# Prompt attention: the outputs of two heads leave PSUM together

## The reference

```python
s = (einsum('bqhd,bkhd->bhqk', qn, k_nope) + einsum('bqhr,bkr->bhqk', qr, k_rope)) * ATTN_SCALE
s = where(mask, s, -inf)
p = softmax(s)
return einsum('bhqk,bkhd->bqhd', p, v)          # head size 128, 256 queries
```

## Time and profile before

| | us |
|---|---|
| median of 3 runs (lowest, highest) | 1997.17 (1993.77, 1998.15) |
| the profiled execution's own time | 1997.47 |
| its span, first to last instruction | 1995.4 |
| PE busy | 1962.7 (98%) |
| DVE busy | 1092.1 (55%) |
| ACT busy | 761.0 (38%) |
| mean granted TensorE clock | 0.995 of full speed |
| the loop of the prompt's attention | from 608.4 to 673.9 |

### The profile page before, as it was taken

How to read it: one execution, slowest core, us unless ns; L and a number is a source line. 1 busy time by engine, 2 the same in 40 slices (tenths; PEclk the granted TensorE clock), 3 DMA queues, 4 the chain that set the end, 5 groups by cost and what they waited for, 6 DMA issues and landing times.

```text
span 1995.4 us, 33957 instructions
## 1 busy us (share of the span) xinstructions
PE 1962.7 (98%) x13378; PEld 1938.4 (97%) x13378; DVE 1092.1 (55%) x1464; ACT 761.0 (38%) x834; POOL 45.0 (2%) x188
## 2 busy tenths in 40 slices
PE   8999999999999999999999999999999999999996
PEld 7999999999998799999999999999999999999996
DVE  6865344333335764355556555555556555565656
ACT  5356542332246654233333232332323333333334
POOL 0002000000000000000000000000000000000000
PEclk9999999999999999999999999999999999999998
DMA  7444444444444388454444434444444444343442
GB/s 247 145 150 168 153 147 147 147 147 148 149 175 161 129 284 278 154 201 149 152 153 145 165 137 159 147 147 147 147 148 148 152 153 151 134 164 142 152 147 103
DMA packets 59575, 318.15 MB, mean 159 GB/s; under 512 B 6466, under 2 KB 6658, under 8 KB 26882
## 3 DMA queue, kind: packets, MB, share of 16 engines
q1 hardware_dynamic: 58866, 313.15, 44.2%
q10 hardware_dynamic: 656, 4.27, 0.5%
HBM read 313.08 MB, written 4.32 MB: 159 GB/s over the span
## 4 chain that ended last, share of the span: by engine, by line
PE 96%; ACT 2%; DVE 2%; issue 0%; DMA 0%; DVEq 0%; SPq 0%; ACTq 0%
PE ps L1342 95%; ACT w_hi L469 0%; PE ps L1628 0%; DVE w_lo L816 0%; ACT sq L795 0%; ACT y_gain L796 0%; DVE sq L816 0%; DMA xT<-in_x 0%; DVE y_gain L816 0%; ACT sm L672 0%; DVE neg_max L1109 0%; DVE sm L1103 0%; ACT pt L469 0%; DVE scale_in L883 0%; PE ps L1574 0%
## 5 line engine op out<-in xcount | busy, mean ns | idle before, releaser
L816 DVE TENSOR_TENSOR w_lo<-w_raw,w_hi 128x2048 fp32r<-128x2048 f32 (+1 forms) x270 | 610.2, 2260 | 459.2 <-ACT w_hi L469 459.0
L1342 PE MATMUL ps<-h_hi,w_hi 128*128 128x320 f32 x2512 | 742.0, 308 | 11.0 <-ACT w_hi L469 11.0
L469 ACT ACTIVATE w_hi<-w_raw 128x2048 fp32r<-128x2048 f32 (+1 forms) x271 | 509.1, 1879 | 630.4 <-PE ps L1342 630.0
L1342 PE MATMUL ps<-h_lo,w_hi 128*128 128x320 f32 x2512 | 740.9, 309 | 0.0
L1342 PEld LDWEIGHTS ps<-h_hi,w_hi 128*128 128x128 f32 x2512 | 473.0, 188 | 11.6 <-ACT w_hi L469 11.2
L1342 PEld LDWEIGHTS ps<-h_lo,w_hi 128*128 128x128 f32 x2512 | 471.5, 188 | 0.2
L1342 PE MATMUL ps<-h_hi,w_lo 128*128 128x320 f32 x2512 | 393.6, 308 | 0.0
L1342 PEld LDWEIGHTS ps<-h_hi,w_lo 128*128 128x128 f32 x2512 | 374.8, 187 | 0.0
L1342 PE MATMUL ps<-hid_hi,w_hi 128*128 128x320 f32 x704 | 216.6, 308 | 1.9 <-DVE x L816 1.9
L1342 PE MATMUL ps<-hid_lo,w_hi 128*128 128x320 f32 x704 | 216.5, 308 | 0.0
L1342 PE MATMUL ps<-hid_hi,w_lo 128*128 128x320 f32 x704 | 216.5, 308 | 0.0
(11 more groups left out here) (226 smaller groups left out, 1763.6 us busy)
## 6 DMA issues: line engine op xcount, KB each, us to landing
w_raw<-in_slabs SPq DMA_DIRECT2D x253, 1024.0 KB, 4.8
w_raw<-in_cache_t SPq DMA_DIRECT2D x64, 288.0 KB, 3.8
c_raw<-in_cache SPq DMA_DIRECT2D x56, 256.0 KB, 4.7
w_whole<-in_slabs SPq DMA_DIRECT2D x4, 1024.0 KB, 8.3
xT<-in_x SPq DMA_DIRECT2D x4, 640.0 KB, 7.4
x_again<-in_x ACTq DMA_DIRECT2D x1, 2560.0 KB, 9.5
out_y<-y_gain SPq DMA_DIRECT2D x4, 640.0 KB, 3.2
c_last<-in_cache SPq DMA_DIRECT2D x8, 256.0 KB, 4.4
```

Source lines behind the costliest of these rows:

```text
L469: return nc.scalar.activation(out, in_, ACT.Copy)
L816: return nc.vector.tensor_tensor(out, a, b, op)
L1342: return nc.tensor.matmul(out, a, b, start=start, stop=stop, **kw)
```

## The change

ACT copies the outputs of two heads, banks 6 and 7, by one instruction in even iterations, and DVE subtracts for two heads by one instruction in odd ones; the value product of head h waits until the pair before its own has been taken.

```diff
@@ ACT
-                if i >= 3:
-                    h = i - 3
-                    act.wait_ge(pv_done, h + 1)
-                    copy(o_hi[:, h, 0:NP], ps[:, 6 + h % 2, 0:NP]).then_inc(ohi_done, 1)
+                if i >= 3 and i % 2 == 0:
+                    h = i - 4
+                    act.wait_ge(pv_done, h + 2)
+                    copy(o_hi[:, h:h + 2, 0:NP], ps[:, 6:8, 0:NP]).then_inc(ohi_done, 1)
@@ DVE
-                if i >= 4:
-                    h = i - 4
-                    dve.wait_ge(ohi_done, h + 1)
-                    tt(o_lo[:, h, 0:NP], ps[:, 6 + h % 2, 0:NP], o_hi[:, h, 0:NP], ALU.subtract).then_inc(olo_done, 1)
+                if i >= 4 and i % 2 == 1:
+                    h = i - 5
+                    dve.wait_ge(ohi_done, h // 2 + 1)
+                    tt(o_lo[:, h:h + 2, 0:NP], ps[:, 6:8, 0:NP], o_hi[:, h:h + 2, 0:NP], ALU.subtract
+                       ).then_inc(olo_done, 2)
@@ PE
                     if h >= 2:
-                        pe.wait_ge(olo_done, h - 1)
+                        pe.wait_ge(olo_done, h - h % 2)
```

## The result

| | before | changed |
|---|---|---|
| median of 4 runs (lowest, highest), us | 1997.14 (1993.77, 1998.15) | 2017.83 (2009.94, 2018.86) |
| ratio, 95% interval | | 1.0101 [1.0088, 1.0115] |
| profiled execution: own time, span | 1997.47, 1995.4 | 2018.27, 2016.2 |
| mean granted clock, as a share of full speed | 0.995 | 0.989 |
| from the loop's first scores to the first product behind it, us | 673.87 - 608.35 = 65.5 | 695.74 - 607.77 = 88.0 |

The kernel became 20.7 us slower (1.0%). The forecast was 2014 us in a range of 2006 to 2028.

A forecast was written before the change was run, and what follows sets the result against it. PE, busy 98% of the span, was taken as the bound. Stalls and tail less waits given back made +10.9 us, two clock falls +5.8: +16.7 on 1997.5, forecast 2014 us, range 2006 to 2028.

The forecast's parts named there:

- The stall and its place: PE's value product of an even head waits for DVE's pair, behind the same iteration's masked scores: 2.37 us, six times.
- The sum at full clock: Loop and tail without clock falls: six stalls +14.2, tail +3.1, today's waits given back -3.9 and -2.5; +10.9 us.
- The tail: Last heads: PE waits 1.4 us at i = 17 and 1.7 us after the last product, +3.1 us.
- The saving: Merged subtractions save DVE 0.15 us a pair, 1.2 over the loop; nothing up to i = 8, later at most 1.2.
- What stands behind the moved instructions: Work queued on ACT and DVE behind the moved copies and subtractions shifts only by tenths of a us.
- The clock: In the loop, the granted clock falls at two of the six new stalls, 2.9 us each: +5.8 us.
- Rival (b): Clock falls at four to six of the loop's stalls, +27 to +30 us in all, up to 2027; chance 0.23.
- The fall behind the loop: Today's clock fall after the tail's two waits was left as it is, because the tail's waits stay alike.
- one to three falls: The forecast's own case: one to three clock falls at the loop's stalls, 2011 to 2018 us; chance 0.41.
- Rival (a): Same stalls in the loop but the clock holds, no fall: 2008 us; chance 0.30.
- (c): Not slower: PE reaches the even head's value product after the wait would end, only -0.8 saved, 1996.4 us; chance 0.03.
- (d): Half of the stalls absorbed where DVE is the bound: +5, 2002 us; chance 0.03.

The follow-up runs named there:

- filled kernel: Changed kernel with ten matmuls of unused result ahead of PE's wait at each even head from 2 to 12, filling the stalls; 2005.53 us.
- ACT's pair alone: Kernel before with only ACT's copy merged; DVE subtracts head by head in its old places and PE has the old wait; 2003.35 us, ratio 1.0036.
- changed again: The changed kernel run once more with nothing altered, for the spread of its runs; 2016.2 us, ratio 1.0096.
- pair first: Changed kernel with DVE's subtraction of the pair moved to the head of the odd iteration, ahead of the wait for the scores; 1999.32 us.
- other work first: Changed kernel with PE's latent queries (i = 5, 7) and next stage's scores (i = 11, 15) put ahead of the value product and its wait; 2002.16 us.

## Why the prediction was right, and where it was off

- **The stall and its place.** Forecast 2.37 us at each of six even heads; measured 2.3 to 2.4 by the matmul rows, 2.48 from start to start in iteration 5. Moving the pair's subtraction ahead of the masked scores removed four of them, and one changed wait made them without any merge. Right.
- **The sum at full clock.** +10.9, from +14.2 and +3.1 less 3.9 and 2.5. The filled kernel measures it: +10.7 in the loop. The tail was forecast at 1.4 and 1.7 us, and is 1.25 and 1.57. Right. (By its own terms the upper bound is 14.2 + 3.1 - 2.8 - 2.3 = 12.2 and not 12.0, and its terms make eight waits of PE and not nine; the changed kernel has eight, six of 2.3 to 2.4 us. Five of them stand in the list of waits under ACT's `pt`, by the coincidence named above.)
- **The saving.** A pair's subtraction was taken at 0.69 (0.68) and its copy at 0.59 (0.58), with no gain on the path. Right; DVE's busy time did not even fall in total.
- **What stands behind the moved instructions** was said to move by tenths of a us. That holds for the change as made, but not by much: ACT's pair alone costs 6 us, because there DVE meets it in the same iteration.
- **The clock, the term that was mis-sized.** The step was "I take two" falls, at 2.9 us each, +5.8. Measured: a loss of 12.0 us, behind every one of the six stalls except that at 677, so five falls of 2.4 us on average. The count was too low and the price of one too high. The price came from the fall behind the loop, which lasted 6.8 us; three of the five lasted 3.4 us and cost 1.7 each. Rival (b) had the count, but at 2.6 to 3.2 a fall, and so 2027.
- **The fall behind the loop** was left as it is. It became half as long (1.7 us lost in place of 3.4), and is absent in six other profiles of the table. In four of these (changed again, stalls filled, pair first, other work first) the tail's waits are at least as long as before the change and were not filled, so its coming and going is not explained.

In all: 10.7 + 12.0 - 1.7 = 21.0 against 20.8 measured by the spans, where the forecast had 10.9 + 5.8 = 16.7. The mechanism was as described, but the number owes something to luck: the case that the forecast stood on, one to three falls, is not what happened. It was rival (b)'s, five falls, and the time stayed below 2018 only since most of them were short. Rival (a), the clock holds, fell with the profile; (c) and (d) fell with the six stalls at full length.

## What to carry to other kernels

Merging the evacuations of two alternating PSUM banks turns a double buffer into a single one: look at which iteration of the reader the writer now waits in, and at what stands ahead of the reader's instruction there. Where a merge is wanted, put the merged instruction ahead of the wait on the writer's newest result, or give the writer other work ahead of its wait; here that took back 18.5 and 15.7 of 20.7 us. Count a stall of TensorE not at its length alone: here the clock about doubled the loss (12.0 us beside 10.7).

## What was not expected of the hardware

- A single idle time of 2.3 to 2.4 us of PE, between stretches in which it was busy, was followed by a fall of the clock from 2.4 to 1.2 GHz in five of six cases in one profile of the changed kernel and in four of six in another. Two of 0.56, one of 0.45 and one of 0.92 us (other work first) were followed by none.
- Length alone does not tell. In the kernel before, waits of 1.25 and 1.02 us were followed by a fall of 6.8 us; 1.25 and 1.57 us by one of 3.4 us in one profile of the changed kernel and by none in the other; 2.52 and 1.58 us (pair first) by none. What decides, the experiments leave open.
- With products of no use in the same gaps the clock stayed at 1.00 through the loop, and the kernel was 12.3 us faster (2017.8 to 2005.5) while its value products waited just as long for DVE.
- In and behind the loop, phases at 1.2 GHz lasted 3.4, 6.8 or 10.2 us, and cost half of that. The same kernel has groups of run times, about 1994.6 and 1997.4 before the change, 2009.7 and 2017 after it, with the higher mean clock in the faster group; that a fall more or less makes the difference is likely, but no run of a faster group was profiled.
